# One interleaved, skewed schedule for the RWKV-7 recurrence of a two-layer decoder block

## The chip, the cores and the metric

The kernel runs on one core of a Trainium2 chip. The metric is the device time of one execution in microseconds (us). The core's engines each work through a queue of their own in order: PE (TensorE, the matrix engine), DVE (VectorE), ACT (ScalarE), POOL (GpSimd) and SP (SyncE, which here only starts DMAs). They meet at semaphores. PE writes only to PSUM, which has eight banks of 512 fp32 values on each of 128 partitions; DVE and ACT carry results from there to SBUF.

## What is computed

A decoder block with two layers over 16 meta tokens and 256 tokens, width 1024. Layer 0 is windowed attention and a dense feed-forward; layer 1 is RWKV-7 time mixing and a mixture of 8 experts (top 2). The change is inside the time mixing. Its core is a recurrence per head (16 heads of 64):

```python
def step(S, inp):
    r_t, w_t, k_t, v_t, a_t, b_t = inp
    sa = jnp.einsum('bhvk,bhk->bhv', S, a_t)
    S = S * w_t[:, :, None, :] + sa[..., None] * b_t[:, :, None, :] + v_t[..., None] * k_t[:, :, None, :]
    return S, jnp.einsum('bhvk,bhk->bhv', S, r_t)
_, out = lax.scan(step, S0, xs)
```

After it come a per-head group norm, a bonus term, a gate and the output projection `w_o`; then the router and the experts. All is fp32.

## The kernel before

The 272 tokens, padded by 48 in front, are cut into `NCH` = 5 chunks of `CH` = 64. The 16 heads lie as `PAIRS` = 8 pairs, the two heads of a pair on the two halves of the 128 partitions (`HROWS`). Instead of 272 steps each chunk is solved with matrices of 64x64 per head. Three stages follow one another, and PE waits between the first and the second until every result of the first has been read:

1. **Groups.** Per chunk PE makes seven groups of products: `BA` and `KA` (`products`: per head the decayed keys against queries and removal keys), `TB`, `TK`, `TV` (`turned`: token-major copies, `TB` and `TK` scaled by the diagonal `Dg`), and, for the chunk before, `RV` and `KV` (`from_values`). There are 32 groups, each of 16 head products in two PSUM banks. Group g uses banks 2*(g % 4) and the next one, so it waits for the reader of group g-4 (`group`). DVE reads `BA` and `KA` (line 2241 for chunks 1 to 4, line 2245 for chunk 0), and then prepares each chunk's first 2x2 block inverse: it adds the unit to `BAa[c]` (line 2249), multiplies by a mask into `XT` (line 2252) and transposes that into `X` (line 2254). ACT reads the other five kinds (lines 1753, 1757, 1760).
2. **Levels.** The unit triangular matrix of each chunk is inverted by doubling the block size: 3 levels for chunk 0 (it holds 16 tokens), 5 for each other chunk, `NLV`; 23 units (level, chunk) in all. A unit is `level_y` on PE (line 1124, 16 head products), a masked copy of the result to `Y` by DVE (line 2262), `level_x` on PE (line 1139), a copy to `X` by ACT (line 1766) and, but for a chunk's last level, a transpose `XT<-X` by DVE (line 2268). The order is level by level: all chunks' `level_y`, then all chunks' `level_x`. `level_y` rotates through banks 0 to 3, `level_x` through banks 4 to 7. In both, every product reads one half of the partitions and writes the same half.
3. **Serial chunks.** Chunk by chunk: `rhs_state` (line 1175), add (DVE, line 2306), `solve` (line 1183), copy (ACT, line 1792), `state_u` (line 1191), add (DVE, line 2315), and for the next chunk's state two more DVE operations on SBUF alone (lines 2318, 2321). Around them PE accumulates the outputs in banks 6 and 7 (`out_open`, `out_state`, `out_values`, `out_u`). Outputs of chunks 1 and 2 are normed (`gn_squares`, `gn_sums`, `gn_root`, `gn_scaled`) before PE reopens the same two banks for chunks 3 and 4 (`pe.wait_ge(yn_ok, 1)`).

Meanwhile POOL scales `bonus` and `g_a` for the gate: 8 operations of line 644, one of line 646, 8 of line 648, then it signals `gb_ok`, which DVE wants in `gated(0)`. On SP the second half of `w_o` (slot 1) is loaded once the last projection with `w_r` has been made (`pr_mm`); all later loads (the row `gainrow` and the expert weights) wait for `ot_mm` 2, the last output of the recurrence. What follows the recurrence is the output projection (line 1269), the router, and the expert loop (lines 1391 to 1393), which ends the program.

Of the kernel before, what the change touches and what calls it, by code (L numbers as in the profile page):

```python
# [24 lines left out]
P = 128  # L25
# [13 lines left out]
CH = 64  # L39
# [31 lines left out]
def build(nc, x, meta_tokens, mixer_norm, ffn_norm, attn_w_qkv, attn_q_norm, attn_k_norm, attn_sinks, attn_w_o,  # L71
# [4 lines left out]
    with ctx:  # L76
# [103 lines left out]
        def area(off, *dims):  # L180
# [56 lines left out]
        Dg = area(X4, NCH - 1, PAIRS, CH)  # L237
        X = area(X4 + 7168, PAIRS * NCH, CH)
        XS = wk + 4608
        XT = area(XS, PAIRS * NCH, CH)  # L240
# [4 lines left out]
        assert XS + 2560 + 2 * FIRST <= X4 and X4 + 7168 + 2560 <= UT + 2176 and UT + 2176 + 3 * FIRST <= ARR  # L245
# [42 lines left out]
        dg_bonus_ok, grp_mm, grp_dve, grp_act, x0_ok, y_mm, y_ev, x_mm, x_act, xt_sd_dve = [sem(n) for n in (  # L288
            "dg_bonus_ok", "grp_mm", "grp_dve", "grp_act", "x0_ok", "y_mm", "y_ev", "x_mm", "x_act", "xt_sd_dve")]
# [114 lines left out]
        NY, NX, NXT = {}, {}, {}  # L404
        for l in range(max(NLV)):
            for c in range(NCH):
                if l < NLV[c]:
                    NY[l, c] = NX[l, c] = len(NY)
                    if l < NLV[c] - 1:
                        NXT[l, c] = len(NXT)  # L410
        LEVELS = sorted(NY)
# [3 lines left out]
        def _(sp):  # L415
# [108 lines left out]
        def _(pool):  # L524
# [115 lines left out]

            pool.wait_ge(dg_bonus_ok, 2)
# [11 lines left out]
        def _(pe):  # L653
# [397 lines left out]
            def group(kind, c):  # L1051

                g = G[kind, c]
                if g >= 4:
                    by_act, n = EVICTED[g - 4]
                    pe.wait_ge(grp_act if by_act else grp_dve, n)
                return 2 * (g % 4)
# [36 lines left out]
            pe.wait_ge(dec_done, PAIRS)  # L1094
            pe.wait_ge(pr_ev, 24)
            pe.wait_ge(rk_ev, PAIRS)
            pe.wait_ge(dg_bonus_ok, 1)
            for c in range(NCH):
                products("BA", c)
                products("KA", c)  # L1100
                if c < NCH - 1:
                    turned("TB", c)
                    turned("TK", c)
                turned("TV", c)
                if c:
                    from_values("RV", c - 1)
                    from_values("KV", c - 1)
            from_values("RV", NCH - 1)


            pe.wait_ge(grp_dve, n_dve)
            pe.wait_ge(grp_act, n_act)

            def level_y(l, c):
                n = NY[l, c]
                if n >= 4:
                    pe.wait_ge(y_ev, n - 3)
                if l:
                    pe.wait_ge(x_act, NX[l - 1, c] + 1)
                else:  # L1120
                    pe.wait_ge(x0_ok, c + 1)
                for p in range(PAIRS):
                    for rows in HROWS:
                        last = mm(ps[rows, n % 4, p * CH:(p + 1) * CH], BAa[c][rows, p, :], X[rows, c * PAIRS + p, :],  # L1124
                                  start=True, stop=True)
                last.then_inc(y_mm, 1)

            def level_x(l, c):
                n = NX[l, c]
                if n >= 4:  # L1130
                    pe.wait_ge(x_act, n - 3)
                pe.wait_ge(y_ev, NY[l, c] + 1)
                if l:
                    pe.wait_ge(xt_sd_dve, NXT[l - 1, c] + 1)
                for p in range(PAIRS):
                    for rows in HROWS:
                        o = ps[rows, 4 + n % 4, p * CH:(p + 1) * CH]
                        x_, y_ = XT[rows, c * PAIRS + p, :], Y[rows, c, p, :]
                        last = mm(o, y_, x_, start=True, stop=True) if l == NLV[c] - 1 else mm(o, x_, y_, start=True, stop=True)  # L1139
                last.then_inc(x_mm, 1)  # L1140

            for l in range(max(NLV)):
                for c in range(NCH):
                    if l < NLV[c]:
                        level_y(l, c)
                for c in range(NCH):
                    if l < NLV[c]:
                        level_x(l, c)
# [17 lines left out]
            def zeros(e):  # L1166

                return ident[HROWS[e], HROWS[1 - e]]

# [8 lines left out]
            def solve(c, y):  # L1178
                pe.wait_ge(x_act, NX[NLV[c] - 1, c] + 1)
                if c:  # L1180
                    pe.wait_ge(rhs_ev, 2 * c - 1 + y)
                for p, e, rows, toks in by_y[y]:
                    last = mm(quarter(2, p, toks), XT[toks, c * PAIRS + p, :], (RHS if c else KAa[0])[toks, p, :], start=True, stop=True)
                last.then_inc(u_mm, 1)

            def state_u(c, y):
                if c == 0:
                    pe.wait_ge(x_act, len(NX))
                pe.wait_ge(u_ev, 2 * c + y + 1)
                for p, e, rows, toks in by_y[y]:  # L1190
                    last = mm(quarter(4, p, rows), b_a[toks, p, cs_(c)], U[c % 2][toks, p, :], start=True, stop=True)
                last.then_inc(s_mm, 1)

            def out_at(c, p, e):
                return ps[HROWS[tok(p, (c - 1) % 2)], 6 + e, p * CH:(p + 1) * CH]
# [5 lines left out]
            def out_open():  # L1201
# [1324 lines left out]
```

## Time and profile before

| | |
|---|---|
| median of 3 runs | 1644.57 us (1642.06 to 1644.63) |
| profiled execution, its time | 1641.22 us |
| profiled execution, its span | 1639.3 us |
| PE busy | 1612.4 us, 98% |
| PE weight loads busy | 1385.2 us, 84% |
| DVE busy | 1251.4 us, 76% |
| ACT busy | 979.6 us, 60% |
| POOL busy | 103.9 us, 6% |
| chain that ended last | PE 94%, DVE 3%, ACT 2% |

The span runs from the first to the last instruction of the profiled execution. Times within it are microseconds from its start. The groups run from 517.3 to 546.2, the levels from 546.9 to 592, the serial chunks from about 591 until PE reopens the output banks at 612.83. Records of matmuls overlap, since they are pipelined, so a busy PE is not PE at its peak; each fp32 product leaves two records, which makes 32 records of one group or half unit. A row of the timeline merges instructions of a kind that follow closely ("x32").

### The profile page before, as it was taken

Reading aid. Unit: us, or ns where it says so; the run is one execution under the profiler, and the core shown is the slowest. Engines: PE = TensorE matmul, PEld = TensorE weight load, DVE = VectorE, ACT = ScalarE, POOL = GpSimd, SP = SyncE. Lnnn points to the kernel's source line nnn. Section 1 sums busy time; section 2 is a strip of 40 time slices with the busy share of each in tenths; the row PEclk is TensorE's granted clock in tenths of the full one; section 3 lists DMA queues with packets and bytes.
Section 4 is the critical chain, followed back from the end, with each engine's and each line's share of the span. In section 5 each row is a group of like instructions: output and inputs, shape, how many; then the busy total and the mean of one; then the engine's idle time right before and its main releaser. Section 6 shows DMA issues by size and latency. Waiting matters only on the chain.

```text
span 1639.3 us, 27733 instructions
## 1 busy us (share of the span) xinstructions
PE 1612.4 (98%) x11475; PEld 1385.2 (84%) x11475; DVE 1251.4 (76%) x1181; ACT 979.6 (60%) x992; POOL 103.9 (6%) x152
## 2 busy tenths in 40 slices
PE   9999999999998989999999999999999999999998
PEld 7889999999787985888888888888888888888887
DVE  5665655535686655888988988888898988898998
ACT  5765434431433333777677676777776767776766
POOL 3473000001003100000000000000000000000000
PEclk9999999999999999999999999999999999999999
DMA  8115555543440006699999999999999999999996
GB/s 286 53 53 183 177 180 181 174 142 102 155 147 10 4 4 244 222 380 373 370 348 352 375 360 373 370 348 357 364 363 378 365 345 359 368 366 374 368 361 222
DMA packets 191616, 432.67 MB, mean 264 GB/s; under 512 B 10051, under 2 KB 11075, under 8 KB 191492
## 3 DMA queue, kind: packets, MB, share of 16 engines
q1 hardware_dynamic: 191452, 430.82, 73.3%
q8 instruction: 92, 1.51, 0.4%
q14 instruction: 32, 0.26, 0.0%
q10 hardware_dynamic: 40, 0.08, 0.0%
HBM read 429.82 MB, written 1.05 MB: 263 GB/s over the span
## 4 chain that ended last, share of the span: by engine, by line
PE 94%; DVE 3%; ACT 2%; issue 1%; POOL 0%; DVEq 0%; ACTq 0%; POOLq 0%
PE ps L1391 18%; PE ps L1393 18%; PE ps L1392 18%; PE ps L722 6%; PE ps L724 6%; PE ps L723 6%; PE ps L974 4%; PE ps L1269 2%; PE ps L1415 1%; PE ps L1124 1%; PE ps L1139 1%; PE ps L984 1%; PE ps L660 1%; PE ps L1344 1%; DVE arena L2241 0%
## 5 line engine op out<-in xcount | busy, mean ns | idle before, releaser
L2427 DVE TENSOR_TENSOR wsplit<-raw_w,wsplit 128x2048 fp32r<-128x2048 f32 x336 | 751.6, 2287 | 77.8 <-ACT wsplit L1842 77.8
L1842 ACT ACTIVATE wsplit<-raw_w 128x2048 fp32r<-128x2048 f32 x336 | 625.1, 1918 | 59.6 <-PE ps L1393 59.6
L1391 PE MATMUL ps<-wsplit,xsplit 128*128 128x512 f32 x896 | 354.4, 396 | 0.2 <-DVE wsplit L2427 0.2
L1393 PE MATMUL ps<-wsplit,xsplit 128*128 128x512 f32 x896 | 349.6, 390 | 0.0
L1392 PE MATMUL ps<-wsplit,xsplit 128*128 128x512 f32 x896 | 348.8, 389 | 0.0
L1393 PEld LDWEIGHTS ps<-wsplit,xsplit 128*128 128x128 f32 x896 | 168.1, 188 | 36.0
L1391 PEld LDWEIGHTS ps<-wsplit,xsplit 128*128 128x128 f32 x896 | 168.3, 188 | 33.8 <-DVE wsplit L2427 0.9
L1392 PEld LDWEIGHTS ps<-wsplit,xsplit 128*128 128x128 f32 x896 | 168.5, 188 | 33.1
L1391 PE MATMUL ps<-wsplit,hsplit 128*128 128x512 f32 x448 | 175.1, 391 | 0.0
L1392 PE MATMUL ps<-wsplit,hsplit 128*128 128x512 f32 x448 | 174.4, 389 | 0.0
L1393 PE MATMUL ps<-wsplit,hsplit 128*128 128x512 f32 x448 | 174.4, 389 | 0.0
L1879 ACT ACTIVATE arena<-ps 128x512 f32<-128x512 f32 x56 | 33.6, 600 | 178.4 <-PE ps L1393 178.3
L2094 DVE TENSOR_TENSOR ffn_lo<-ffn_raw,ffn_hi 128x2048 fp32r<-128x2048 f32 x42 | 95.0, 2293 | 54.9 <-ACT ffn_hi L1647 54.7
L724 PE MATMUL ps<-u_hi,ffn_lo 128*128 128x272 f32 x448 | 129.0, 288 | 0.0
L722 PE MATMUL ps<-u_hi,ffn_hi 128*128 128x272 f32 x448 | 128.9, 288 | 0.0
L723 PE MATMUL ps<-u_lo,ffn_hi 128*128 128x272 f32 x448 | 128.9, 288 | 0.0
L1647 ACT ACTIVATE ffn_hi<-ffn_raw 128x2048 fp32r<-128x2048 f32 x42 | 78.6, 1904 | 37.8 <-PE ps L724 37.8
L1393 PEld LDWEIGHTS ps<-wsplit,hsplit 128*128 128x128 f32 x448 | 84.1, 188 | 17.6
L1391 PEld LDWEIGHTS ps<-wsplit,hsplit 128*128 128x128 f32 x448 | 84.1, 188 | 17.0
L1392 PEld LDWEIGHTS ps<-wsplit,hsplit 128*128 128x128 f32 x448 | 84.1, 188 | 16.9
L722 PEld LDWEIGHTS ps<-u_hi,ffn_hi 128*128 128x128 f32 x448 | 84.6, 189 | 0.1
L723 PEld LDWEIGHTS ps<-u_lo,ffn_hi 128*128 128x128 f32 x448 | 84.2, 188 | 0.1
(412 smaller groups left out, 2236.4 us busy)
## 6 DMA issues: line engine op xcount, KB each, us to landing
raw_w<-in_moe_w_gate SPq DMA_DIRECT2D x114, 1024.0 KB, 6.9
raw_w<-in_moe_w_up SPq DMA_DIRECT2D x112, 1024.0 KB, 7.8
raw_w<-in_moe_w_down SPq DMA_DIRECT2D x112, 1024.0 KB, 7.1
ffn_raw<-in_ffn_w_up SPq DMA_DIRECT2D x14, 1024.0 KB, 5.1
ffn_raw<-in_ffn_w_gate SPq DMA_DIRECT2D x14, 1024.0 KB, 5.1
ffn_raw<-in_ffn_w_down SPq DMA_DIRECT2D x14, 1024.0 KB, 5.1
ffn_raw<-in_attn_w_qkv SPq DMA_DIRECT2D x6, 1024.0 KB, 11.7
ffn_raw<-in_attn_w_o SPq DMA_DIRECT2D x4, 1024.0 KB, 11.0
```

What stands on the lines that cost most here:

```text
L722: mm(o, w_hi_, x_hi_, start=first, stop=False)
L723: mm(o, w_hi_, x_lo_, start=False, stop=False)
L724: return mm(o, w_lo_, x_hi_, start=False, stop=last_)
L974: last = mm(ps[:, j % 4, cols_], slot_k[s][:, k, (m % 4) * P:(m % 4 + 1) * P], xm[(0, 1, 0)[which]][:, k, cols_], start=(k == 0), stop=(k ...
L1391: mm(o, x_[0], w_[0], start=first_, stop=False)
L1392: mm(o, x_[0], w_[1], start=False, stop=False)
L1393: return mm(o, x_[1], w_[0], start=False, stop=last_)
L1647: A(ffn_hi[:, m % NFH, :], ffn_raw[:, ffn_at(m), :], ACT.Copy).then_inc(hi_ok, 1)
L1842: A(wsplit[:, m % NRING, 0, :], raw_w[:, m % NRAW, :], ACT.Copy).then_inc(w_hi, 1)
L1879: A(hbuf[:, q % 2, :], ps[:, q % 2, :], ACT.Silu).then_inc(e_silu, 1)
L2094: v.tensor_tensor(ffn_lo[:, ffn_at(m), :], ffn_raw[:, ffn_at(m), :], ffn_hi[:, m % NFH, :].bitcast(F32), ALU.subtract).then_inc(lo_ok, 1)
L2427: v.tensor_tensor(wsplit[:, m % NRING, 1, :], raw_w[:, m % NRAW, :], wsplit[:, m % NRING, 0, :].bitcast(F32), ALU.subtract).then_inc(w_lo, 1)
```

## The change

The three stages become one. A tick t issues the groups of chunk t, and for each chunk c whose inverse is under way level t-1-c (`units(t)`); from tick 5 on the serial steps of the chunks are put among the levels, so that chunk 0 is solved in tick 5, chunk 1 in tick 7, then one per tick. With this:

- Banks are divided: groups use banks 0 to 3 (two slots, so a group waits for the reader of g-2), `level_y` banks 4 and 5 (one slot), `level_x` banks 6 and 7 (one slot; in ticks 5 and 6 every second unit uses banks 2 and 3), the serial steps banks 0 and 1, the outputs banks 2 and 3 for chunks 1 and 2 and banks 6 and 7 for chunks 3 and 4.
- In the levels the products of odd pairs write the other half of the partitions. `X[c]` and `XT[c]` hold 12 slots: 4 to 11 the matrices by parity, 0 to 3 the odd ones once more with halves swapped. ACT makes the swapped copies (`first_sides` from SBUF, four copies of 64x256; in `take_x` two copies of 64 partitions x 128 from PSUM).
- But for the last level of a chunk, DVE and ACT carry only the columns that a level changes: half of them (`even`).
- The unit and the mask of the first blocks move from DVE to POOL (two operations of 128x512 per chunk, ahead of POOL's `bonus` work); DVE transposes only (`first_turned`). `gb_ok` now counts them too.
- `Dg` moves to slot 1, and the load of the second half of `w_o` into that slot also waits for the group `TK` of chunk 3. ACT's preparation for the square root is issued ahead of the groups, and the wait on `yn_ok` ahead of the second `out_open` is gone.

The diff, cut to its core:

```diff
-        Dg = area(X4, NCH - 1, PAIRS, CH)
-        X = area(X4 + 7168, PAIRS * NCH, CH)
+        Dg = area(SLOT0 + SLOT, NCH - 1, PAIRS, CH)
+        X = [area(X4 + 7168 + c * SIDES, 3 * PAIRS // 2, CH) for c in range(4)] + [area(W_A, 3 * PAIRS // 2, CH)]
...
+        def units(t):
+            return [(t - 1 - c, c) for c in range(NCH) if 0 <= t - 1 - c < NLV[c]]
+        XBANK = {u: 2 if t in (NCH, NCH + 1) and i % 2 else 6 for t in range(TICKS) for i, u in enumerate(units(t))}
+        def even(v, l):
+            b = 2 << l
+...
+            return v.rearrange("p a (j x i) -> p a j x i", x=2, i=b)[:, :, :, 0, :]
...
+                if w is rwkv_w_o and n == 1:
+                    sp.wait_ge(grp_mm, G["TK", NCH - 2] + 1)
                 load(s, slot_k[s], cols(w[0], n))
...
+            for c in range(NCH):
+                pool.wait_ge(grp_dve, EVICTED[G["BA", c]][1])
+                one(g.tensor_tensor(BAa[c], BAa[c], mask64[:, 8, :].unsqueeze(1).to_broadcast([P, PAIRS, CH]), ALU.add))
+                own.done(g.tensor_tensor(XT[c][:, 4:12, :].rearrange("p (y q) i -> p y q i", y=2), by_parity(BAa[c]),
+                                         mask64[:, 7, :].unsqueeze(1).unsqueeze(1).to_broadcast([P, 2, 4, CH]), ALU.mult), gb_ok)
             pool.wait_ge(dg_bonus_ok, 2)
...
-                if g >= 4:
-                    by_act, n = EVICTED[g - 4]
+                if g >= 2:
+                    by_act, n = EVICTED[g - 2]
...
             def level_y(l, c):
-                n = NY[l, c]
-                if n >= 4:
-                    pe.wait_ge(y_ev, n - 3)
+                n = NTH[l, c]
+                if n:
+                    pe.wait_ge(y_ev, n)
...
-                for p in range(PAIRS):
-                    for rows in HROWS:
-                        last = mm(ps[rows, n % 4, p * CH:(p + 1) * CH], BAa[c][rows, p, :], X[rows, c * PAIRS + p, :],
-                                  start=True, stop=True)
+                for q in range(PAIRS // 2):
+                    for y in range(2):
+                        for a, rows in enumerate(HROWS):
+                            last = mm(ps[HROWS[a ^ y], 4 + y, q * CH:(q + 1) * CH], BAa[c][rows, 2 * q + y, :],
+                                      X[c][rows, 4 + 4 * y + q, :], start=True, stop=True)
...
+            for t in range(NCH):
+                U_ = units(t)
+                if U_: level_y(*U_[0])
+                products("BA", t)
+                if len(U_) > 1: level_y(*U_[1])
+                products("KA", t)
+                if U_: level_x(*U_[0])
+                if t < NCH - 1: turned("TB", t)
+                if len(U_) > 2: level_y(*U_[2])
+                if t < NCH - 1: turned("TK", t)
+                if len(U_) > 1: level_x(*U_[1])
+                turned("TV", t)
+                if t: from_values("RV", t - 1)
+                if len(U_) > 2: level_x(*U_[2])
+                if t: from_values("KV", t - 1)
+            U_ = units(5)
+            from_values("RV", NCH - 1)
+            level_y(*U_[0]); level_y(*U_[1]); level_x(*U_[0])
+            solve(0, 0); solve(0, 1)
+            level_y(*U_[2]); level_x(*U_[1]); level_y(*U_[3])
+            state_u(0, 0); state_u(0, 1)
+            level_x(*U_[2]); level_x(*U_[3])
...
+            U_ = units(9)
+            solve(3, 0); solve(3, 1)
+            level_y(*U_[0])
+            state_u(3, 0); state_u(3, 1)
+            level_x(*U_[0])
+            rhs_state(4, 0); rhs_state(4, 1)
+            solve(4, 0); solve(4, 1)
+            out_open(6)
...
+            def take_x(l, c):
...
+                A(even(X[c][:, 4:12, :], l), even(ps[:, b:b + 2, 0:4 * CH], l), ACT.Copy).then_inc(x_act, 1)
+                for a, rows in enumerate(HROWS):
+                    last = A(even(X[c][HROWS[1 - a], 0:4, :], l), even(ps[rows, b + 1, 0:4 * CH], l), ACT.Copy)
+                last.then_inc(x_flip, 1)
...
+            for t in range(NCH):
+                U_ = units(t)
+                if U_: masked(*U_[0])
+                taken("BA", t)
+                if len(U_) > 1: masked(*U_[1])
+                taken("KA", t)
+                if len(U_) > 2: masked(*U_[2])
+                for u in U_[:2]: turned(*u)
+                first_turned(t)
+                for u in U_[2:]: turned(*u)
+            U_ = units(5)
+            masked(*U_[0]); masked(*U_[1]); masked(*U_[2])
+            turned(*U_[0])
+            masked(*U_[3])
+            state_added(0)
+            turned(*U_[1])
+            state_kept(0)
+            turned(*U_[2]); turned(*U_[3])
```

The first loop over t above is PE's order in ticks 0 to 4, the second DVE's; what follows each loop is the same engine's tick 5 (for PE tick 9 too), and `take_x` is ACT's. `taken` is DVE's read of `BA` or `KA`, `masked` the masked copy after `level_y`, `turned` (on DVE) the transpose, `state_kept` the two operations of lines 2318 and 2321. Several calls that the diff has on lines of their own stand on one line here. ACT's order in ticks 0 to 4 is: `first_sides` of the chunk before, `take_x` of the first unit, `TB`, `TK`, `take_x` of the second, `TV`, `RV`, `take_x` of the third, `KV`.

## Rows read from the trace of the kernel before

**Rows 1.** The page: busy time, share of the span, instructions; granted clock by fortieths.

```profile
PE 1612.4 (98%) x11475; PEld 1385.2 (84%) x11475; DVE 1251.4 (76%) x1181; ACT 979.6 (60%) x992; POOL 103.9 (6%) x152
PEclk9999999999999999999999999999999999999999
```

**Rows 2.** Windows: length, busy PE, PEld, DVE, ACT, POOL; granted clock, DMA share, GB/s.

```profile
517.30:546.20 28.90, 23.40 (x1024) 21.74 (x1024) 23.02 (x34) 11.48 (x22) 20.24 (x17) 1.00 0.02 5
546.80:592.00 45.20, 44.88 (x1503) 44.46 (x1504) 28.17 (x41) 13.79 (x24) 0.00 (x0) 1.00 0.02 4
592.00:612.80 20.80, 15.57 (x591) 14.21 (x587) 12.94 (x26) 6.33 (x15) 0.00 (x0) 1.00 0.01 3
...
650.00:1639.00 989.00, 982.80 (x4521) 815.23 (x4519) 866.68 (x555) 709.52 (x529) 0.00 (x0) 1.00 0.96 351
```

**Rows 3.** Timeline, first groups: start, us, engine, line, operation, shapes, count [idle before <-releaser].

```profile
517.30 1.16 PE L1071 MATMUL ps<-arena 64*64 64x64 f32 x64 [0.53 <-issue]
...
518.06 0.69 DVE L2245 TENSOR_TENSOR arena<-ps,mask 128x512 f32<-128x512 f32 x1
...
520.13 2.13 PE L1069 MATMUL ps<-arena 64*64 64x128 f32 x62 [0.26 <-DVE arena L2245]
```

**Rows 4.** Timeline, first level: `level_y` of five chunks on PE.

```profile
546.89 4.88 PE L1124 MATMUL ps<-arena 64*64 64x64 f32 x160 [0.75 <-issue]
```

**Rows 5.** Groups of instructions from 517 to 613, by shape: busy us, mean ns | idle before, releaser.

```profile
L1124 PE MATMUL ps<-arena 64*64 64x64 f32 x736 | 23.1, 218 | 0.8 <-issue 0.8
...
L2262 DVE TENSOR_TENSOR arena<-ps,mask 128x512 f32<-128x512 f32 x23 | 15.7, 685 | 5.7 <-PE ps L1124 5.7
L1766 ACT ACTIVATE arena<-ps 128x512 f32<-128x512 f32 x23 | 13.7, 597 | 31.4 <-PE ps L1139 31.4
L2268 DVE STREAM_TRANSPOSE arena<-arena 128x512 f32<-128x512 f32 x18 | 12.8, 712 | 8.0 <-ACT arena L1766 8.0
...
L1792 ACT ACTIVATE arena<-ps 128x256 f32<-128x256 f32 x10 | 3.7, 381 | 12.9 <-PE ps L1183 12.5
...
L2306 DVE TENSOR_TENSOR arena<-arena,ps 128x256 f32<-128x256 f32 x8 | 3.1, 419 | 0.5 <-PE ps L1175 0.3
...
L1788 ACT ACTIVATE mstat<-normcol 128x1 f32<-128x1 f32 x1 | 0.2, 203 | 0.0
```

**Rows 6.** Timeline, serial chunks: `solve`, two ACT copies, and the reopening of the banks.

```profile
593.35 0.64 ACT L1792 ACTIVATE arena<-ps 128x256 f32<-128x256 f32 x2
593.86 0.80 PE L1191 MATMUL ps<-arena 64*64 64x64 f32 x26 [1.63 <-ACT arena L1792]
...
602.31 0.97 PE L1183 MATMUL ps<-arena 64*64 64x64 f32 x26 [0.85 <-DVE arena L2306]
...
607.24 1.21 PE L1183 MATMUL ps<-arena 64*64 64x64 f32 x32 [1.32 <-DVE arena L2306]
...
610.96 1.15 PE L1183 MATMUL ps<-arena 64*64 64x64 f32 x32
...
612.83 1.09 PE L1205 MATMUL ps<-mask,ident 64*64 64x512 f32 x8 [0.71 <-DVE arena L2285]
```

**Rows 7.** Groups of POOL's instructions, by shape: the eight of line 644.

```profile
L644 POOL TENSOR_SCALAR arena<-arena,par 128x256 f32<-128x256 f32 x8 | 7.7, 983 | 107.3 <-DVE arena L2224 107.3
```

**Rows 8.** Timeline: DVE beside POOL's operations.

```profile
518.25 7.72 POOL L644 TENSOR_SCALAR arena<-arena,par 128x256 f32<-128x256 f32 x8 [107.33 <-DVE arena L2224]
518.78 0.69 DVE L2249 TENSOR_TENSOR arena<-arena,mask 128x512 f32<-128x512 f32 x1
...
526.05 4.54 POOL L646 TENSOR_TENSOR arena<-arena 128x2048 f32<-128x2048 f32 x1
...
527.65 1.29 DVE L2241 TENSOR_TENSOR arena<-ps,mask 128x512 f32<-128x512 f32 x2 [1.74 <-PE ps L1069]
...
528.97 2.17 DVE L2249 TENSOR_TENSOR arena<-arena,mask 128x512 f32<-128x512 f32 x1
```

**Rows 9.** Timeline: the load of `w_o`.

```profile
470.20 15.48 SPq L420 DMA_DIRECT2D arena<-in_rwkv_w_o  x2
```

More of the change, by code:

```diff
@@ new lines, in _ @@
+            U_ = units(5)
+            from_values("RV", NCH - 1)
+            level_y(*U_[0])
+            level_y(*U_[1])
+            level_x(*U_[0])
+            solve(0, 0)
+            solve(0, 1)
+            level_y(*U_[2])
+            level_x(*U_[1])
+            level_y(*U_[3])
+            state_u(0, 0)
+            state_u(0, 1)
+            level_x(*U_[2])
+            level_x(*U_[3])
+            U_ = units(6)
+            level_y(*U_[0])
+            level_y(*U_[1])
+            level_x(*U_[0])
@@ new lines, in _ @@
+            rhs_state(1, 0)
+            rhs_state(1, 1)
+            level_y(*U_[2])
+            level_x(*U_[1])
+            level_y(*U_[3])
+            level_x(*U_[2])
+            level_x(*U_[3])
+            U_ = units(7)
+            solve(1, 0)
+            solve(1, 1)
+            level_y(*U_[0])
+            x_read(units(6)[1])
+            x_read(units(6)[3])
+            out_open(2)
+            out_state(1)
+            level_y(*U_[1])
+            level_x(*U_[0])
+            state_u(1, 0)
@@ new lines, in _ @@
+            state_u(1, 1)
+            pe.wait_ge(own_mm, own_at["out", 1])
+            out_values(1, (0, 1))
+            level_y(*U_[2])
+            level_x(*U_[1])
+            signal_own(out_u(1, (0, 1)), ("u", 1))
+            rhs_state(2, 0)
+            rhs_state(2, 1)
+            level_x(*U_[2])
+            U_ = units(8)
+            solve(2, 0)
+            solve(2, 1)
+            level_y(*U_[0])
+            pe.wait_ge(own_mm, own_at["u", 1])
+            out_state(2)
+            level_y(*U_[1])
@@ new lines, in _ @@
+            level_x(*U_[0])
+            state_u(2, 0)
+            state_u(2, 1)
+            pe.wait_ge(own_mm, own_at["out", 2])
+            out_values(2, (0, 1))
+            level_x(*U_[1])
+            out_u(2, (0, 1)).then_inc(ot_mm, 1)
+            rhs_state(3, 0)
+            rhs_state(3, 1)
+            U_ = units(9)
+            solve(3, 0)
+            solve(3, 1)
+            level_y(*U_[0])
+            state_u(3, 0)
+            state_u(3, 1)
+            level_x(*U_[0])
+            rhs_state(4, 0)
@@ new lines, in _ @@
+            U_ = units(7)
+            masked(*U_[0])
+            masked(*U_[1])
+            state_added(1)
+            masked(*U_[2])
+            rhs_added(2)
+            turned(*U_[0])
+            turned(*U_[1])
+            state_kept(1)
+            turned(*U_[2])
+            U_ = units(8)
+            masked(*U_[0])
+            masked(*U_[1])
+            state_added(2)
+            rhs_added(3)
+            turned(*U_[0])
+            turned(*U_[1])
+            state_kept(2)
+            gn_sums(0)
@@ L2324, in _ @@
+            masked(*units(9)[0])
+            state_added(3)
+            rhs_added(4)
+            gn_scaled(0)
             dve.sem_inc(w_lo, NRAW)
```

375 lines of the change are left out of this document (210 added, 165 removed).

## The prediction

> **What bounds the kernel now.** I read the page first: PE is busy for 98% of the span and its granted clock stands at the top level throughout [rows 1], so a gain must come out of PE's own queue, as fewer idle spots or as the same products issued faster; nothing is to be had from the clock. The windows by stage come next [rows 2]. The expert loop is PE's alone (982.8 of 989.0 us) and the change doesn't touch it. The recurrence lies before it and hides behind nothing, so a microsecond saved there is one off the end, provided that the loop's own start moves along. It does: all expert loads wait for the recurrence's last output, so they start earlier by the same amount. Within the recurrence the groups take 28.9 us with PE busy 23.4 and DVE 23.0, the levels 45.2 with PE busy 44.9 and DVE only 28.2, the serial chunks 20.8 with PE busy 15.6 (latency). From the first product at 517.30 [rows 3] to the reopening of the output banks at 612.83 [rows 6] it is **95.5 us**. I count this stretch again in the new order, t = 0 at the first product.
>
> **Prices.** PE: 64 records (two groups) take 1.16 us [rows 3]; the last product needs 0.22 us to finish (the mean of one record [rows 5], subtracted here), so (1.16-0.22)/64 = 14.7 ns each: a group of 32 issues in 0.47 and is complete at 0.69. The levels have the same product shape but 160 records in 4.88 us [rows 4]: 29.1 ns, 0.93 a half unit. What differs is where they write. The groups spread over all four combinations of input half and output half, the levels over two; so does `solve`, one parity at a time, and it too has 32 in 1.15 [rows 6]. Since the new levels use all four combinations, I price a half unit at 0.47. Products of 128 columns: 62 records in 2.13 [rows 3], 0.96 a group. DVE: 0.69 for 512 columns, 0.42 for 256, 0.71 a transpose; ACT 0.60 and 0.38 [rows 5]. The swapped copies (64 partitions x 128) aren't in the trace; they lie between 0.20 (one column) and 0.38 (256 columns) [rows 5], I take 0.27, by the slope of ACT's rows. The second of two ACT copies starts 0.26 after the first [rows 6], so a `take_x` is 0.65 to 0.7 and `first_sides` 1.2. POOL: 128x512 isn't there. A quarter of line 646 is 1.14 [rows 8]; two operations of line 644 are 1.97 for the same columns [rows 7]. I take 1.35, near the first, as it is the same kind of operation: 2.8 us for the pair (ends 2.3 and 3.9). Handovers: PE complete at 517.98, DVE starts at 518.06 [rows 3], 0.1; the first ACT copy ends at 593.73, PE starts at 593.86 [rows 6], 0.15.
>
> Such a count can be tried on a stretch that is there: a serial chunk with outputs comes to 5.0 us, the trace has 607.24-602.31 = 4.93; the last one comes to 4.0 against 610.96-607.24 = 3.72 [rows 6]. So it errs, if at all, to the long side by a few per cent.
>
> **Work on each engine.** PE: 10 product groups 8.6, 22 others 10.3, 46 half units 21.6 (before: 46 x 0.93 = 42.8), serial products 12.2 and outputs 3.8: 56.5 us. DVE: 18 reads of groups 12.4, 23 masked copies 11.0 (18 of them now 0.42 instead of 0.69), 23 transposes 16.4, serial adds 6.8, `state_kept` 4.2, the norm 2.5: 53 us. It gives 10 operations to POOL, lines 2249 and 2252 (two of them in [rows 8]). ACT: 22 groups 13.2, `take_x` 15.2, `first_sides` 6, the rest 5: 39 us. No engine needs 95.5, so the stretch gets shorter unless waits eat it. PE's 56.5 is the floor.
>
> **Tick by tick.** Tick 0 holds five groups. The first `level_y` stands ahead of the next `BA` in PE's queue and needs the first block: `BA` read at 1.45, POOL's pair to 4.35, transpose to 5.15, so tick 1 starts on PE at 5.3, while the last group of tick 0 is issued at 3.6. PE loses 1.7, and all groups behind that wait with it. Ticks 1 to 4 are set by the two group slots: `TB` waits for DVE's read of `BA` (0.96+0.22+0.1+1.3+0.15), `TV` for ACT's of `TB`, and so on, with the units in the gaps. Following the three queues I get tick ends on PE at 12.2, 20.3, 28.4 and 35.9: about 8 us a tick, with PE's own work 6 to 7.7. By then all groups and 9 units are done; the kernel before needs 29.6 us to the start of its levels, all 23 units still to do. Tick 5 (four units, `solve(0)`, `state_u(0)`) ends on PE at 43.4. Here DVE becomes late: after `state_added(0)` at 43.1 it has `turned`, `state_kept(0)` (1.4), and two more `turned` in its queue before the first masked copy of tick 6, so that starts at 46.7 where PE has delivered at 44.1, and the one `level_y` slot makes PE wait. Ticks 6, 7 and 8 then end at 52.6, 60.7 and 68.8, and the last `solve` at **76.7**; in these the same pattern (`state_kept` and `turned` ahead of the next masked copy) costs PE 1.5 to 3.5 a tick. The serial chain alone (4.9 a chunk) is no longer what sets them.
>
> **The collision.** One more wait belongs in that sum. POOL's `bonus` work now starts only after the last first block: `BA` of chunk 4 is read at 31.6, the pair ends at 34.4, the eight operations of line 644 at 42.1, and line 646 runs from 42.2 to 46.7. In the trace a DVE operation with two SBUF inputs that comes beside line 646 takes 2.17 us instead of 0.69 and ends 0.55 after it, while one that reads PSUM and a mask runs beside it undisturbed (2 in 1.29), and one beside line 644 takes its 0.69 [rows 8]. `state_kept(0)` has two such operations and comes up at 43.8, in the middle of it. It would end at 48.0 instead of 45.3: 2.7 us, in the tick where DVE is what PE waits for. The bounds of this are 0 (it comes before 42.2 or after 46.7) and 4.5. I take it as happening, since the count leaves 1.6 and 2.9 us on either side: **79.4** to the end of the last `solve`.
>
> The Trainium skill, page "SBUF — State Buffer", section "Who interferes with whom", states the rule behind that: a DVE instruction with two SBUF inputs contends with a GpSimd instruction that reads SBUF, and whichever is second blocks for the whole of the other. By the rule line 644 should block it too, which the row at 518.78 doesn't show; the sum would be the same by rule and by row as long as `state_kept(0)` meets line 646, and up to 1 us worse by the rule if it met an operation of line 644 or 648.
>
> **What else moves.** The load of the second half of `w_o` took at most 15.5 us for both halves [rows 9]; it now starts at about 26 us in the stretch and is needed some 60 us later, with the DMA engines at 2% [rows 2]: nothing. It is alone in the SP queue until the outputs are done. If it weren't covered it would cost its 8 to 15 us. POOL's end of the `bonus` work (54.7, or 57 with slips) comes long before `gated(0)`. The norm of the first half is ready at about 80.5, and PE reaches its transposes some 3.5 us after reopening the banks: nothing. ACT's table load for the square root (1.3 us) falls before the groups instead of between levels and serial chunks; that is in the sum.
>
> **Sum.** 95.5 - 79.4 = 16.1 us less. On the profiled execution 1641.2 becomes 1625.1. The median of the runs lies 3.3 us above the profiled execution; measured against it the forecast is 1644.6 - 16.1 = **1628.5 us**.
>
> **Rivals.**
> 1. *The round trips take back more.* `level_y` and `level_x` now have one slot each, the groups two instead of four. If each of the 8 ticks with units and company loses one more round trip of `level_y` (0.69+0.1+0.42+0.15 = 1.36), 10.9 us go: gain 5.2, **1639.4**. For it: three queues in fixed order, each of which can be late for the others, and DVE as busy as 53 in 79. Against it: the count has these trips in already, and the method came out long on the trace. The skill's page "TensorEngine Tiling (Array Packing)", section "PSUM Bottleneck", says that packing speeds up TensorE but not the emptying of PSUM; by that the levels would go at the pace of DVE and ACT, which is this case.
> 2. *The levels aren't issued faster.* If the 29.1 ns come from something else than the two combinations, 46 x 0.46 = 21.2 us are back on PE, of which the 23 us of waits in my count hide perhaps a half: gain between -5 and 6, middle **1644**. That is the change not doing what it says. Against it: `solve` and the groups, both of shape 64x64.
> 3. *POOL's pair is dear, and it ends slower.* Every chunk's pair P stands before its first level, in a PE queue in order. Chunk 0 has no slack, the other four about 1.7 us. Slower from 5P - 5x2.8 - 4x1.7 = 16, P = 7.4, that is 3.7 us an operation; at 4.5 (as much as line 646 for a quarter of its columns) it would be 9 us slower, **1654**. Against it: both bounds are under 2 us.
> 4. *No collision.* `state_kept(0)` misses line 646, and the count errs long as on the last chunk: gain 19 to 22, **1623 to 1626**.
>
> **How the numbers follow.** Forecast 0.5, rival 4 0.2, rival 1 0.17, rival 2 0.07, rival 3 0.06. The range reaches from rival 4 (22 us less, and 1.5 for the spread of the runs) to rival 1: 1621 to 1640. A measurement of this kernel can tell 0.2% (3.3 us) from no change. Faster by more: the forecast, rivals 4 and 1, less a tail, 0.85; within: most of rival 2, 0.07; slower: rival 3 and the rest, 0.08.
>
> **What would show it.** The levels' 32 records within 0.5 us; 5.3 us from the first product to the first `level_y`; ticks of 8 us; DVE's operation with two SBUF inputs in tick 5 at over 2 us beside line 646; the last `solve` ending 79 us after the first product. Wrong would be: a half unit at 0.93 (rival 2), POOL's operations over 2 us each (rival 3), or PE idle before `level_y` by more than 3 us in ticks 1 to 4 (rival 1).

## The result, and the profile after

The changed kernel took 1644.51 us (median of 20 runs, 1642.23 to 1648.7), the kernel before, beside it, 1642.54 (20 runs, 1640.07 to 1644.68): ratio 1.0014, 95% interval 1.0007 to 1.0020. That is 2 us slower, by the interval 1 to 3, and within the bound of 0.2% no change; the forecast was 16.1 us less. The profiled execution spans 1643.9 us.

From the page after, the busy times and the instruction queue (to be read beside [rows 1]):

```profile
PE 1599.3 (97%) x11475; PEld 1369.5 (83%) x11475; DVE 1237.3 (75%) x1171; ACT 994.5 (60%) x1048; POOL 115.7 (7%) x162
q8 instruction: 92, 1.51, 0.4%
```

PE is busy for 13 us less, with the same 11475 matmuls, in a span that is 4.6 us longer than the 1639.3 of the profiled execution before. So products did get faster, and the time came back as idle PE. The stretch that the prediction counts, first product to second reopening of the output banks, 517.30 to 612.83 before [rows 3, 6], now goes from 517.40 to 614.58: 97.2 us instead of 95.5. Of the 4.6 us that is 1.7; 0.1 lie ahead of it and 2.8 behind it, where the two kernels do the same. A part of those 2.8 is the granted clock, low for some 7 us after and for some 4 before (window, length, PE busy and records, clock, DMA share, GB/s):

```profile
661.00:669.00 8.00, 6.98 (x37) 0.57 0.01 2
```

and before:

```profile
654.00:658.00 4.00, 4.00 (x24) 0.57 0.00 0
```

From the second reopening to the end, the profiled executions of all kernels here need between 1025.8 and 1029.6 us, whatever was changed (1029.3 in the changed kernel, 1026.5 before). So the mechanism is read from the stretch, and what a change is worth in all from the medians.

The stretch's windows after, PE alone (window, length, busy and matmul records, granted clock, DMA share, GB/s):

```profile
517.40:613.00 95.60, 67.14 (x3076) 0.96 0.08 26
530.24:533.77 3.53, 2.91 (x128) 1.00 0.02 5
533.77:537.12 3.35, 2.51 (x128) 1.00 0.02 5
537.12:540.87 3.75, 2.68 (x127) 1.00 0.02 4
540.87:544.87 4.00, 2.89 (x128) 1.00 0.01 4
544.87:548.87 4.00, 2.09 (x128) 1.00 0.26 63
548.87:555.25 6.38, 2.56 (x127) 1.00 0.78 294
```

and the same window before:

```profile
516.80:613.00 96.20, 84.03 (x3116) 1.00 0.02 4
```

84.0 us of PE work became 67.1, as the price of 14.7 ns promised, and 28.5 us of the 95.6 are idle. What ended that idle time (PE's waits from 517.4 to 613: line waited for, us in total, times, longest):

```profile
PE ps L1165 <- issue: 4.5, 5, 1.2
PE ps L1138 <- issue: 4.3, 2, 3.8
PE ps L1124 <- issue: 3.7, 3, 1.9
PE ps L1138 <- DVE arena L2384: 3.5, 2, 3.1
```

All rows of "issue" together are 21.0 us, those of DVE and ACT 7.5. So the largest releaser is none of the engines. "issue" is time in which PE waits for nothing that the profile shows. The timeline tells where it falls:

```profile
529.41 0.38 PE L1138 MATMUL ps<-arena 64*64 64x64 f32 x8
530.24 0.52 PE L1138 MATMUL ps<-arena 64*64 64x64 f32 x20 [0.45 <-issue]
...
532.80 0.35 PE L1165 MATMUL ps<-arena 64*64 64x64 f32 x8
533.77 0.58 PE L1165 MATMUL ps<-arena 64*64 64x64 f32 x24 [0.62 <-issue]
534.16 1.15 PE L1124 MATMUL ps<-arena 64*64 64x64 f32 x64
```

PE stops in the middle of a half unit, after 8 or 9 of 32 records, where no semaphore can hold it. The six windows above are cut at the ends of seven such stops in a row: each holds 127 or 128 matmuls, hence 128 weight loads too, whatever lines they belong to. The DMA view of 530.24 to 544.87, four of these windows, has four packets and no others:

```profile
GB/s 0 0 0 45 0 0 0 0 0 0 0 0 45 0 0 0 0 0 0 0 0 0 45 0 0 0 0 0 0 0 0 0 0 45 0 0 0 0 0 0
q8 instruction: 4, 0.07, 1.6%
```

One packet of the instruction queue, 1.51 MB / 92 = 16 KB, belongs to each 128 records of products with their 128 loads. The four lie near 531.5, 534.8, 538.5 and 542.4, each 2.2 to 2.5 us ahead of the end of a stop (533.77, 537.12, 540.87, 544.87). From 587.57 to 609.83, where six more blocks end, a period is 22.26 / 6 = 3.71 us; the four above take 14.63 / 4 = 3.66. The kernel before has such packets too, in its levels (547 to 590) one in 43 / 11 = 3.9 us:

```profile
q8 instruction: 11, 0.18, 1.8%
```

The Trainium skill, page "Runtime: NRT & Kernel Launch", section "Instruction fetch mechanics", says that instructions are fetched in blocks of 16 KiB, 256 of them. That agrees with 128 and 128 to a packet. It also says that the cost of crossing into the next block is mostly hidden; here it is not, with stops of 0.3 to 1.9 us, and 3.8 once.

**Theory F** (instruction supply). PE gets 256 instructions about every 3.7 us (3.35 to 4.0 in the windows without the load). The stretch has about 3110 records, 24.3 blocks, 24.3 x 3.71 = 90 us, in any order; this is an estimate by the mean pace. Before, the levels at 29.1 ns a record need 128 x 29.1 ns = 3.73 us a block, by chance the pace of the supply, so it hardly showed there. Crossing the halves moves PE from its own pace to the supply's, which is the same.

In the groups of the kernel before, whose records are as cheap as the new ones, it did show, small beside the waits for DVE, and the prediction overlooked it:

```profile
529.22 0.98 PE L1091 MATMUL ps<-arena 64*64 64x64 f32 x51 [0.58 <-issue]
...
540.72 1.76 PE L1069 MATMUL ps<-arena 64*64 64x128 f32 x56 [0.65 <-issue]
...
544.38 0.62 PE L1083 MATMUL ps<-arena 64*64 64x64 f32 x25 [0.40 <-issue]
```

Counted from the first product, PE resumes there with the records 458, 840 and 967 (and with 713 after 0.47 us). In the changed kernel it resumes with 457, 584, 711, 838, 965 and 1092, though the products there come in another order. So the place in the instruction stream decides, in steps of 127, and not which product it is.

**Theory W** (rivals 1 and 2 in one): waits of the engines for each other in the new order, and the price of each product, set the 97 us; the stops are a small part beside them.

### The profile page after: what moved, and what is told of

Same layout as the page of the kernel before. It is cut to its first block, busy times and chain, and to the rows that moved or that the text cites. A ratio compares the mean times of both kernels' runs of the same rounds, so it can differ in the third digit from the quotient of the medians.

```text
span 1643.9 us, 27798 instructions
## 1 busy us (share of the span) xinstructions
PE 1599.3 (97%) x11475; PEld 1369.5 (83%) x11475; DVE 1237.3 (75%) x1171; ACT 994.5 (60%) x1048; POOL 115.7 (7%) x162
## 3 DMA queue, kind: packets, MB, share of 16 engines
q8 instruction: 92, 1.51, 0.4%
## 4 chain that ended last, share of the span: by engine, by line
PE 93%; DVE 2%; issue 2%; ACT 2%; POOL 0%; DVEq 0%; ACTq 0%; POOLq 0%
PE ps L1489 18%; PE ps L1491 18%; PE ps L1490 18%; PE ps L755 6%; PE ps L757 6%; PE ps L756 6%; PE ps L1007 4%; PE ps L1367 2%; PE ps L1513 1%; PE ps L1017 1%; PE ps L1138 1%; PE ps L1442 1%; PE ps L1165 1%; PE ps L693 1%; PE ps L1102 0%
```

## The experiments

The stretch below is always from the first product to the first record of the second reopening, in the profiled execution. But for experiment 8, its start lies between 516.2 and 519.5 from one execution to the next, with nearly the same code ahead of it, so stretches are compared and not ends.

**1. Does the load of `w_o` cost nothing?** The changed kernel, with `Dg` in the area that `uT` leaves, so that the load need not wait:

```diff
-        Dg = area(SLOT0 + SLOT, NCH - 1, PAIRS, CH)
+        Dg = area(UT, NCH - 1, PAIRS, CH)
...
-                if w is rwkv_w_o and n == 1:
-                    sp.wait_ge(grp_mm, G["TK", NCH - 2] + 1)
```

> Changed kernel with one part undone: the diagonals Dg lie where uT was (dead by then) instead of in slot 1, so the second half of w_o is loaded as early as before the change. Theory F (instruction supply): in the changed kernel PE stops in the middle of groups, waiting for nothing that the profile shows, every 128 matmul records (128 records and their weight loads), at best every 3.7 us; that sets the stretch. Under it the load of w_o beside the recurrence stretched two such periods (4.0 and 6.4 us), and PE's granted clock fell after the 3.8 us stop. Expected: the 6.4 us period becomes 3.7, the clock keeps its level there, 3 to 5 us less than the changed kernel, so 1 to 3 us less than the kernel before; the other periods stay at 3.4 to 4.0 us. Theory W (waits for the single bank slots and for late DVE): w_o has no part in it, the same as the changed kernel within 1 us.

Measured: 1642.49 us (11 runs), ratio 1.0008 (0.9999 to 1.0018). In the changed kernel the load is issued at 546.58, in the ticks, and PE has its longest stop behind it:

```profile
546.58 0.37 SPq L443 DMA_DIRECT2D arena<-in_rwkv_w_o  x1
```

```profile
548.87 0.62 PE L1124 MATMUL ps<-wide,arena 64*64 64x64 f32 x26 [1.91 <-issue]
...
551.14 0.28 PE L1138 MATMUL ps<-arena 64*64 64x64 f32 x2
555.25 0.69 PE L1138 MATMUL ps<-arena 64*64 64x64 f32 x27 [3.83 <-issue]
...
555.82 1.93 PE L1102 MATMUL ps<-arena 64*64 64x128 f32 x31
```

With the load at 484.15 the same place reads:

```profile
548.08 0.62 PE L1122 MATMUL ps<-wide,arena 64*64 64x64 f32 x26 [1.91 <-issue]
...
551.99 0.63 PE L1136 MATMUL ps<-arena 64*64 64x64 f32 x27 [1.36 <-issue]
...
552.50 1.04 PE L1100 MATMUL ps<-arena 64*64 64x128 f32 x30
```

The period of 6.38 is 3.91, and the products after it don't run at half pace. The other stops remain. The stretch is 611.74 - 516.15 = 95.6 us, 1.6 shorter. By the medians the kernel gains 2.0 us, by the ratios 1 to 3 (1.0008 against 1.0014, whose intervals overlap, and 1.0025 when the changed kernel was run again); F had 3 to 5, W less than 1. So the load costs 1 to 3 us, and isn't what took the 16.

**2. Does a product's price depend on its columns?** The kernel before, with the level products but the last of a chunk on the half of the columns that is read later, in the same number (`level_x`, DVE's masked copy and ACT's copy are changed likewise):

```diff
-                        last = mm(ps[rows, n % 4, p * CH:(p + 1) * CH], BAa[c][rows, p, :], X[rows, c * PAIRS + p, :],
+                        last = mm(part(ps[rows, n % 4, p * CH:(p + 1) * CH]), BAa[c][rows, p, :], part(X[rows, c * PAIRS + p, :]),
```

> Kernel before with only this: in all levels but a chunk's last, PE, DVE and ACT work on the changed half of the columns (32 instead of 64 per product, the same number of products). Same order, banks and halves. Theory F: PE still needs its 1472 level records at 3.7 us per 128, 42.6 us less the one or two blocks it has ahead: the levels go from 45.2 to 40 to 43 us, stops without a releaser appear in them, the whole is 2 to 4 us faster. Theory W (no limit from the supply): PE's 18 two-sided units halve to about 17 us and the last ones stay at 9, DVE has 24 us: the levels take 28 to 32 us, the whole is 13 to 17 us faster.

Measured: 1645.06 us (12 runs, 1639.99 to 1660.26), ratio 1.0054 (1.0024 to 1.0083). The excess rests on five executions near 1660; the median of the other seven is 1643.2. The stretch is 614.92 - 516.80 = 98.1, 2.6 longer. First level:

```profile
547.43 4.86 PE L1131 MATMUL ps<-arena 64*64 64x32 f32 x160 [0.75 <-issue]
```

160 records of 32 columns take 4.86 us, those of 64 took 4.88 [rows 4], both without a stop inside. Neither theory had this right: a product of this size has a price that doesn't fall with its columns, so the experiment removed no time from PE and can't tell F from W by its total. F had also said that stops without a releaser would appear in the levels; some did, small ones (the kernel before has one, of 0.15 us):

```profile
564.86 2.00 PE L1149 MATMUL ps<-arena 64*64 64x32 f32 x63 [0.42 <-issue]
```

Why five executions lay near 1660 stays open.

**3. The load beside products in the kernel before.** Only the wait of the changed kernel's SP queue is added:

```diff
+                if w is rwkv_w_o and n == 1:
+                    sp.wait_ge(grp_mm, G["TK", NCH - 2] + 1)
```

> Kernel before with only the wait of the second w_o half on the group TK of chunk 3 added, so the 2 MB load runs beside the last groups. Theory F: one supply period is stretched from 3.7 to about 6.4 us, 1.5 to 3.5 us slower, visible as a stop of PE without a releaser near 545 to 550. Theory W: nothing, within 0.5 us.

Measured: 1647.2 us (7 runs), ratio 1.0035 (1.0022 to 1.0049), stretch 616.48 - 517.31 = 99.2, 3.7 longer:

```profile
543.14 0.28 PE L1085 MATMUL ps<-arena 64*64 64x64 f32 x5
546.29 0.62 PE L1085 MATMUL ps<-arena 64*64 64x64 f32 x25 [2.87 <-issue]
```

In the kernel before, the stop at this very place (7 of the 32 records done, 544.38 above) is 0.40 us long. In a schedule that is otherwise unchanged it is now 2.87, and there is nothing but the load to make it so. The rest of the 3.7 is mostly the clock, which is at half for about 4 us behind this stop: the first 160 level records take 6.43 us instead of 4.88. F had 1.5 to 3.5 us slower, W nothing; the median is 5.1 above that of the kernel before. With experiment 1 this shows that a transfer of 2 MB holds up the supply of PE. In the changed kernel no packet of the instruction queue comes between 546.6 and 552.5, while the load runs.

**4. The level products one-sided again.** The changed kernel, each level product written to the half that it reads, as before the change (in `level_x` likewise, with the slots of `XT` and its transpose to match):

```diff
-                            last = mm(ps[HROWS[a ^ y], 4 + y, q * CH:(q + 1) * CH], BAa[c][rows, 2 * q + y, :],
+                            last = mm(ps[HROWS[a], 4 + y, q * CH:(q + 1) * CH], BAa[c][rows, 2 * q + y, :],
```

> Changed kernel with the level products writing the half of the partitions that they read (two combinations of halves instead of four), as in the kernel before; the swapped copies are still made and not used. Theory F: a level half unit goes from 0.47 to 0.93 us of PE, but 128 records at 29 ns are 3.7 us, the supply period itself, so most of it is hidden: 0 to 4 us slower than the changed kernel. Theory W: PE is held only by its own work and by waits, so the 21 us of added PE work show at least by half, 10 to 20 us slower.

Measured: 1647.13 us (6 runs), ratio 1.0038 (1.0024 to 1.0053), stretch 615.85 - 517.11 = 98.7. My prices say that this takes 46 x 0.46 = 21.2 us back. It takes 1.5 on the stretch (97.2 in the changed kernel), and by the ratios to the kernel before (1.0038 against 1.0014 and 1.0025 for the changed kernel) 2 to 4 us of the whole. F had 0 to 4, W 10 to 20. So the faster product is worth next to nothing here: what PE gains in a half unit it stands still for at the next block.

**5. Half of the level products left out.** The changed kernel, `q` over two pairs instead of four in `level_y` and `level_x`. 736 records less, all evictions, copies and waits stay:

```diff
-                for q in range(PAIRS // 2):
+                for q in range(PAIRS // 4):
```

> Changed kernel in which each half unit of the levels makes 8 of its 16 head products; the others are left out, so the inverses of half of the heads are not computed. ACT and DVE do all they did. 736 of some 3110 matmul records go between the first product and the second out_open (97.2 us apart in the changed kernel). Theory F (PE is supplied with 128 matmul records and their weight loads per 3.7 us): 5.75 blocks less, 15 to 21 us off the stretch and off the time. Theory W (waits for single bank slots and late DVE): PE had 30 us of idle time in the stretch and its own work falls by 10.8 us; DVE and ACT and their waits stay: 1 to 6 us off.

**6. The value groups made twice.** `TV`, `RV` and `KV`, 448 more records, and no operation more on any other engine:

```diff
-                for p, e, rows, toks in heads:
+                for p, e, rows, toks in heads + heads:
...
-                for p, e, rows, toks in heads:
+                for p, e, rows, toks in heads + (heads if kind == "TV" else []):
```

> Changed kernel in which the 14 groups TV, RV and KV make every product twice, to the same place with the same result. 448 more matmul records, 3.5 blocks; nothing else is added on any engine. Theory F: 12 to 14 us longer. Theory W: PE's own work grows by 14 x 0.47 = 6.6 us, into idle time of 30 us: 0 to 4 us longer.

**The changed kernel again**, on the same chip, to compare these two and the next with:

> The changed kernel as it is, on the same chip as the three beside it. Both theories: 0.1 to 0.2% slower than the kernel before, the stretch 96 to 98 us.

Measured: 1646.39 us (10 runs), ratio 1.0025 (1.0015 to 1.0034), stretch 617.36 - 519.43 = 97.9. Against it experiment 5 with 1626.27 (4 runs, ratio to the kernel before 0.9908, 0.9891 to 0.9924) is 20.1 us less, and experiment 6 with 1656.67 (4 runs, 1.0094, 1.0077 to 1.0111) 10.3 more. W had 1 to 6 and 0 to 4, F 15 to 21 and 12 to 14, so experiment 5 came out by F, and experiment 6 between the two, nearer F. In these groups PE had gaps that W says would swallow the products; they didn't. Both differences are also more than all that the products need on PE, 736 x 14.7 ns = 10.8 us and 448 x 14.7 ns = 6.6. PE's windows over the stretches of 5 and 6:

```profile
517.20:596.50 79.30, 57.68 (x2365) 0.96 0.09 30
```

```profile
519.30:625.50 106.20, 76.06 (x3553) 0.98 0.08 24
```

Blocks times 3.71 against the stretch: experiment 5 has 18.5 blocks, 68.6 us of 79.5; the changed kernel 24.3, 90.2 of 97.2; experiment 6 27.8, 103 of 106.3. The excess over the supply falls from 11 to 7 to 3. So waits still count where there are few instructions, and the supply nearly alone where there are many; per block the medians give 3.5 us down (20.1 / 5.75) and 2.9 up (10.3 / 3.5).

**7. The waits for DVE.** In tick 6 of the changed kernel PE waits 3.11 us for a masked copy that has the two operations of `state_kept(0)` and two transposes ahead of it, as the prediction had it:

```profile
576.16 0.65 DVE L2444 TENSOR_TENSOR arena<-arena,chunkdecay 128x512 f32<-128x512 f32 x1
576.85 0.85 DVE L2447 TENSOR_TENSOR arena<-arena 128x512 f32<-128x512 f32 x1
577.73 1.31 DVE L2397 STREAM_TRANSPOSE arena<-arena 128x512 f32<-128x512 f32 x2
578.96 0.65 DVE L2384 TENSOR_TENSOR arena<-ps,mask 128x512 f32<-128x512 f32 x1
```

```profile
579.67 0.60 PE L1138 MATMUL ps<-arena 64*64 64x64 f32 x12 [3.11 <-DVE arena L2384]
```

On top of experiment 1 the first masked copies of ticks 6, 8 and 9 go ahead of such work (the cut shows ticks 6 and 8):

```diff
-            state_kept(0)
-            turned(*U_[2])
-            turned(*U_[3])
-
+            held = U_
...
+            turned(*held[2])
...
+            turned(*held[3])
+            state_kept(0)
...
-            state_kept(1)
-            turned(*U_[2])
-
+            held = U_
...
+            turned(*held[2])
+            state_kept(1)
```

> The kernel of e1 (diagonals elsewhere, early w_o load) with another order on DVE: in ticks 5 to 9 the masked copies for which PE waits come ahead of state_kept, of the late transposes and of the norm's sums. It takes away the 3.1 us stop before a level_y in tick 6. Theory F: the supply runs on while PE waits for DVE, so PE only stops later for lack of instructions instead: 0 to 1.5 us faster than e1. Theory W: 3 to 6 us faster than e1.

Measured: 1640.56 us (10 runs), ratio 0.9991 (0.9981 to 1.0000), and on another chip once more:

> The kernel of e7 once more, beside e10 on the same chip: 1640 to 1642 by both theories, ratio 0.999 to 1.000.

1640.52 (11 runs), ratio 0.9997 (0.9988 to 1.0006). Stretches 612.38 - 519.26 = 93.1 and 611.72 - 519.52 = 92.2, 2.5 and 3.4 less than in experiment 1; the medians are 1.9 and 2.0 less. F had 0 to 1.5 us, W 3 to 6: it came between the two, so the waits for DVE do cost something beside the supply. In both stretches the clock stays at the top level. The second one, with its largest waits:

```profile
519.50:611.50 92.00, 65.74 (x3101) 1.00 0.02 4
```

```profile
PE ps L1163 <- issue: 6.1, 7, 1.6
PE ps L1122 <- issue: 3.5, 3, 1.9
PE ps L1197 <- issue: 2.8, 3, 1.2
```

The wait of 3.1 us is gone, and what remains is "issue"; 92.2 lies 2 us above the 90 of the supply. Of the kernels that do all the work it is the fastest here, and no more than even with the kernel before.

**8. Move blocks to where supply is idle.** On top of experiment 7 the groups `BA`, `KA`, `TB`, `TK` of chunks 0 to 3 stand among the last three projections of v, whose products of 272 columns need few instructions. Their banks and their readers move with them, and in the ticks `RV`, `KV` and `TV` come in another order:

```diff
-            for t in range(NCH):
+            for c in range(NCH - 1):
+                products("BA", c)
+                products("KA", c)
+                if c == 0:
+                    pe.wait_ge(dg_bonus_ok, 1)
+                turned("TB", c)
+                turned("TK", c)
+                if c < 3:
+                    project(3 * KC - 3 + c)
```

> Built on the kernel of e7. Of the products that need no state, the four groups BA, KA, TB, TK of the chunks 0 to 3 (16 groups, 512 short matmuls with 512 weight loads) are issued among the last three of the v projections, on banks 4 to 7, instead of in the ticks; the work of TensorE stays the same. The ticks and the stretch behind them keep the rest. Theory F (TensorE is supplied with blocks of 128 matmuls and 128 weight loads at best every 3.7 us): long projection matmuls leave supply idle, so 512 records are four blocks that are no longer in the ticks, but they still cost at their own place what supply takes less what the projection hides; second state output some 6 to 9 us earlier than in e7, kernel 1632 to 1635, ratio 0.993 to 0.996. Theory W (waits of engines for each other and the price of each product set the time): the products cost at their new place what they cost at the old one, 512 x 14.7 ns = 7.5 us less in the ticks and as much more ahead of them, kernel within 2 us of e7, 1639 to 1642. If the groups disturb the projections, both would be slower than e7: 1642 to 1648.

Measured: 1647.67 us (6 runs), ratio 1.0041 (1.0023 to 1.0059): 7.2 slower than the same kernel without it. Neither theory's number; only the case that I had set apart as "disturb". The rest did shrink: the 16 groups and `TV` of chunk 0, 544 records, stand ahead of 537.95, and the banks are reopened at 616.29, 78.3 us for 20.1 blocks, 13.9 less than the 92.2 of experiment 7, 3.3 us for each of the 4.25 blocks taken out. But the new place cost more than that:

```profile
518.16 3.93 PE L1021 MATMUL ps<-arena 128*128 128x272 f32 x16
522.02 1.98 PE L1116 MATMUL ps<-arena 64*64 64x128 f32 x64
524.54 0.69 PE L1138 MATMUL ps<-arena 64*64 64x64 f32 x32 [0.54 <-DVE arena L2407]
525.73 0.69 PE L1138 MATMUL ps<-arena 64*64 64x64 f32 x32 [0.50 <-DVE arena L2407]
526.36 3.93 PE L1021 MATMUL ps<-arena 128*128 128x272 f32 x16
...
537.95 1.87 PE L1128 MATMUL ps<-arena 64*64 64x64 f32 x30 [2.34 <-ACT arena L1894]
```

A chunk there is 4.3 us between two projections: 3.3 of PE's own time, as 64 of its 128 records are of 128 columns and take 31 ns each, and 1.04 of waits for DVE's masks, which have no other work of PE beside them. Then come 2.34 for ACT, after which the clock is at half until about 543.5 (mean of 538 to 616: 0.96). Together 537.95 - 505.96 less three projections of 3.93 is 20.2 us, against the 13.9 saved: 6.3 more, the measured 7. Here nothing was to be had from idle supply, since a chunk's 128 records took 4.3 us at their new place, more than a block's 3.7.

## Why the prediction was wrong, point by point

**The failed step is "PE's 56.5 is the floor".** The sum was made from PE's busy time, the queues of DVE, ACT and POOL, and their handovers. It had no line for the supply of instructions. With that the floor is about 90 (an estimate, 24.3 blocks at the mean pace of 3.71), not 56.5, which leaves some 5.5 us of the 95.5 to any order of the same products; the shortest stretch with all of them was 92.2. The clue was in the trace of the kernel before: the stops of "<-issue" within its groups, which the rows of the prediction leave out. Nothing in the 29.1 ns itself said that the supply had just this pace.

- *Prices of PE: right.* 64 records in 1.15 to 1.16, a half unit in 0.69, as forecast; rival 2 ("not issued faster") is false as a mechanism, though its 1644 is the time that came: luck. POOL's pair took 1.27 and 1.28, against 1.35 (rival 3 false; redone, its sum for 4.5 us an operation gives 8 us slower, not 9). ACT's copies were priced too low: `first_sides` took 1.7 us instead of 1.2 and a `take_x` 1.0 instead of 0.65 to 0.7, which makes ACT busy for 46.4 us instead of 39.
- *Tick 1: right.* First `level_y` at 522.42, 5.0 us in (5.3). Tick 2 at 12.0 (12.2). From tick 3 on, when the blocks of 128 run at the supply's pace, it is late: 21.5 against 20.3, then 33.7 (551.14) against 28.4. Experiments 5 and 6 show why.
- *The load "nothing": wrong.* It does have the SP queue to itself and is there in time; what it meets isn't a queue or a reader but the instruction packets. Experiment 1 has 1 to 3 us for it, experiment 3 in the kernel before 3.7 in the stretch and 5 by the medians.
- *"Nothing is to be had from the clock": not quite.* A digit 9 of [rows 1] covers 41 us. The clock was at half for some 4 us before, behind the stretch (654 to 658), and in the changed kernel for some 4 us each after two long stops in it.
- *The collision: didn't happen.* `state_kept(0)` came at 576.16, POOL's long operation had ended at 573.64. By then all was 15 us late. 2.7 us too many in the sum; rival 4 had the mechanism, not the time. Instead it met the operations of line 681 (line 648 before):

```profile
573.73 7.48 POOL L681 TENSOR_SCALAR arena<-arena,par 128x256 f32<-128x256 f32 x8
```

Beside them its two operations took 0.65 and 0.85 us, against 0.65 and 0.69 alone in tick 8 (at 597.86 and 598.54), and one operation of POOL 1.17 instead of 0.93; when the changed kernel was run again they took 0.91 and 0.87. So a meeting with these costs a fraction of the 1 us that the prediction allowed for it; a meeting with line 679 (line 646 before) happened in no run.
- *Tick 6's wait for DVE: right*, 3.11 us, and worth about 2 to 3 us together with the same order in ticks 8 and 9, by experiments 1 and 7 (ratios 1.0008 and 0.9991, 0.9997).
- *Rival 1* gave 1639.4, with one more round trip a tick. Waits for DVE and ACT are about a quarter of PE's idle time (7.5 us, against 21.0 of "issue").

What stays open: why a block takes 3.7 us to come, when the packet itself moves within one slice of 0.37 us of the DMA view and PE resumes only 2.2 to 2.5 us behind it, and the five executions near 1660 of experiment 2. All experiments that changed the number of instructions changed matmuls with their loads. That it is the instructions, and not something else that PE does once in 127 of them, rests on the packets, on the equal record numbers in different orders, and on what the load does to both; no run varied other instructions.

## What to carry to other kernels

Where TensorE works on products so small that 128 matmul records with their loads take under about 4 us, count blocks of 128 records before counting engines: by this kernel, that count times 3.7 us is about the least that the stretch takes in any order, and fewer instructions, not faster ones, get below it. Look for the sign in the kernel before, ahead of a prediction. The sign in the profile is "<-issue" in the middle of a group, in equal steps of records. Keep large loads out of such a stretch, and before moving short products beside long ones, price their own time and the round trips that they bring along.

## What the runs showed of the hardware

- Among 64x64 products at 14.7 ns a record, PE stands still every 127 or 128 matmul records with as many loads, in periods of 3.35 to 4.0 us, one 16 KB packet of the instruction queue in each, in the four looked at above 2.2 to 2.5 us ahead of the end of the stop.
- A load of 2 MB beside it makes a period 6.38 us long (3.91 without), and a stop 2.87 us long in the other kernel (0.40 without).
- After some stops the granted clock falls, for some microseconds, from 2.4 to 1.2 GHz: in the changed kernel after 3.83 and 3.11 us of standing still the two windows below, in experiment 8 after 2.34 us. In the stretch of experiment 7, with no stop over 1.9 us, it stayed at 1.00. The length of one stop alone doesn't settle it: behind the stretch of the changed kernel it fell at 661 with stops of 0.7 and 1.0 us around it, and in experiment 6 it stayed at 1.00 after 2.03 us.

```profile
555.30:560.00 4.70, 4.70 (x156) 0.64 0.02 3
579.70:584.00 4.30, 4.27 (x160) 0.62 0.01 4
```

- A 64x64 product costs as much with 32 columns as with 64 (4.86 and 4.88 us for 160 records), and twice as much where only two of the four combinations of halves are used (`solve`, 32 in 1.15 [rows 6]) as where all four are (64 in 1.16 [rows 3]).
